# Two blocks of a transformer on one core: the low parts of three weight pieces and of one output piece are made earlier in VectorE's order

## The reference

```python
h = rms_norm_2(x, attn_norm_w[layer])
proj = h @ w_in[layer]
a_q, a_i, a_zf, a_zb, a_g, b_u, c_q, c_k, c_v = jnp.split(proj, SPLIT_POINTS, axis=-1)
o_a = hgrn2_mixer(a_q, a_i, a_zf, a_zb, a_g, lb_all[layer])      # recurrent, 4 heads
o_b = fourier_mixer(b_u)
o_c = dilated_attention_mixer(c_q, c_k, c_v, positions)           # 8 heads of 64
x = x + jnp.concatenate([o_a, o_b, o_c], axis=-1) @ w_out[layer]
h = rms_norm_2(x, mlp_norm_w[layer])
x = x + jnp.square(jax.nn.relu(h @ w_up[layer])) @ w_down[layer]
```

## Time and profile before

| | |
|---|---|
| median of 3 runs | 3080.66 us (3077.87 to 3081.01) |
| the profiled execution, its own time | 3081.01 us |
| span in its trace | 3079.2 us |
| TensorE (PE) busy | 2894.8 us, 94% |
| its weight loads (PEld) busy | 2291.1 us, 74% |
| VectorE (DVE) busy | 2159.4 us, 70% |
| ScalarE (ACT) busy | 1631.3 us, 53% |
| GpSimd (POOL) busy | 161.7 us, 5% |

### The profile page before, as it was taken

One profiled execution on the slowest core, in us unless ns is written; L12 is line 12 of the kernel. 1 busy time (PEld: TensorE's weight loads), 2 busy tenths in 40 slices (PEclk: granted clock), 3 DMA queues, 4 the chain that ended last, 5 costly groups with the idle time before them and its releaser, 6 DMA issues. The chain is left out here.

```text
span 3079.2 us, 40916 instructions
## 1 busy us (share of the span) xinstructions
PE 2894.8 (94%) x13474; PEld 2291.1 (74%) x13474; DVE 2159.4 (70%) x3016; ACT 1631.3 (53%) x2149; POOL 161.7 (5%) x120
## 2 busy tenths in 40 slices
PE   7988987899999999999997799899999998999998
PEld 6746666788888888888885676588887766688887
DVE  5477666999999999999996666554454466554444
ACT  5233553788888888888884435332232334342222
POOL 0000550000000000000002000000000000000000
PEclk9965586999999999999997899999999999999999
DMA  6167674899999999999997321233232321233222
GB/s 237 55 227 252 214 279 170 339 381 381 390 389 387 389 379 383 390 388 387 382 372 283 111 62 35 72 101 102 76 110 96 103 69 33 88 92 103 96 79 93
DMA packets 292110, 660.07 MB, mean 214 GB/s; under 512 B 21306, under 2 KB 145994, under 8 KB 291988
## 3 DMA queue, kind: packets, MB, share of 16 engines
q1 hardware_dynamic: 276178, 603.54, 53.1%
q0 software_dynamic: 10272, 37.04, 3.2%
q10 hardware_dynamic: 5538, 17.87, 1.5%
HBM read 582.86 MB, written 75.50 MB: 214 GB/s over the span
## 5 line engine op out<-in xcount | busy, mean ns | idle before, releaser
L1358 DVE TENSOR_TENSOR weights_low<-pieces,weights_high 128x1024 fp32r<-128x1024 f32 x768 | 891.3, 1219 | 73.8 <-ACT weights_high L1351 64.1
L1351 ACT ACTIVATE weights_high<-pieces 128x1024 fp32r<-128x1024 f32 x768 | 804.8, 1061 | 204.0 <-PE banks L261 203.3
L259 PE MATMUL banks<-weights_high,xT_high 128*128 128x512 f32 x1024 | 403.7, 394 | 1.3 <-DVE weights_low L1358 1.3
L260 PE MATMUL banks<-weights_low,xT_high 128*128 128x512 f32 x1024 | 400.2, 391 | 0.0
L261 PE MATMUL banks<-weights_high,xT_low 128*128 128x512 f32 x1024 | 400.0, 391 | 0.0
L2218 ACT ACTIVATE weights_high<-pieces 128x1024 fp32r<-128x1024 f32 x192 | 200.7, 1053 | 322.2 <-DMA pieces<-in_w_up 249.6
L2222 DVE TENSOR_TENSOR weights_low<-pieces,weights_high 128x1024 fp32r<-128x1024 f32 x192 | 233.5, 1223 | 115.2 <-ACT weights_high L2218 89.9
L259 PE MATMUL banks<-hT_high,weights_high 128*128 128x512 f32 x704 | 281.9, 400 | 2.8 <-DVE hT_low L3244 2.8
L260 PE MATMUL banks<-hT_low,weights_high 128*128 128x512 f32 x704 | 274.5, 390 | 0.0
L261 PE MATMUL banks<-hT_high,weights_low 128*128 128x512 f32 x704 | 274.5, 390 | 0.0
L259 PEld LDWEIGHTS banks<-weights_high,xT_high 128*128 128x128 f32 x1024 | 193.1, 189 | 53.0 <-issue 13.6
(11 more groups left out here) (459 smaller groups left out, 4658.5 us busy)
## 6 DMA issues: line engine op xcount, KB each, us to landing
pieces<-in_w_mlp SPq DMA_DIRECT2D x768, 512.0 KB, 7.5
expert_out<-mask SPq DMA_DIRECT2D x32, 1536.0 KB, 14.7
pieces<-in_w_up SPq DMA_DIRECT2D x64, 512.0 KB, 3.9
pieces<-in_w_down SPq DMA_DIRECT2D x64, 512.0 KB, 3.3
pieces<-in_w_in SPq DMA_DIRECT2D x56, 512.0 KB, 4.8
pieces<-in_w_ada SPq DMA_DIRECT2D x48, 512.0 KB, 5.9
expert_out<-y ACTq DMA_DIRECT2D x32, 512.0 KB, 7.6
pieces<-in_w_out SPq DMA_DIRECT2D x16, 512.0 KB, 4.5
```

The source lines that it names most:

```text
L259: nc.tensor.matmul(out, a[0], b[0], start=start, stop=False)
L260: nc.tensor.matmul(out, a[0], b[1], start=False, stop=False)
L1351: self.core.nc.scalar.activation(self.hi[:, c % E_PARTS, :], self.raw[:, c % E_RAW, :], ACT.Copy).then_inc(self.high.sem, 1)
L1358: self.core.nc.vector.tensor_tensor(self.lo[:, c % E_PARTS, :], self.raw[:, c % E_RAW, :], self.hi[:, c % E_PARTS, :], ALU.subtract).then_ ...
```

## The change

In slots 17, 18 and 19 (where `in_splits` isn't empty and there is something to pass) VectorE's `split` moves ahead of `normalise_probs(i - 1)` and `low_values(i - 2)`. In slot 16 these two do not occur with h = 0. Behind slot 23, `split(layer, P_OUT)` moves ahead of `low_values(layer, 14)`. That makes four moves in a layer and eight in all. ScalarE's list, TensorE's list and the DMAs stay as they are, and nothing is added or removed.

```diff
@@ VectorE, slots 16 to 23, for h in range(2)
                             if s == 23 and h == 0:
                                 rec_gate(layer, 0)
+                            if h == 0:
+                                for p in in_splits[s]:
+                                    split(layer, p)
                             if i >= 1:
                                 normalise_probs(layer, i - 1)
                             if i >= 2:
                                 low_values(layer, i - 2)
-                            if h == 0:
-                                for p in in_splits[s]:
-                                    split(layer, p)
                             if s == 17 and h:
                                 carry(layer, 0)
@@ VectorE, behind slot 23
                     normalise_probs(layer, 15)
+                    split(layer, P_OUT)
                     low_values(layer, 14)
-                    split(layer, P_OUT)
                     split(layer, P_OUT + 1)
```

## The result

| | us |
|---|---|
| kernel before, median of 5 runs | 3080.66 (3075.52 to 3081.20) |
| changed kernel, median of 5 runs | 3105.62 (3095.62 to 3109.59) |
| ratio of the runs, 95% interval | 1.0091 (1.0076 to 1.0106) |
| profiled execution: time, span | 3105.49, 3103.7 |

The forecast was 3105.9 with a range of 3098 to 3112. The ratio stands for 28 us and its interval for 23 to 33 us. The two spans differ by 3103.7 - 3079.2 = 24.5 us. Single times of the changed kernel scatter widely: the record lists 14 executions of it, from 3095.62 to 3113.65 us, with a median of 3107.6 us. That the forecast meets the median of five to 0.3 us is luck.

The account below looks back on a forecast made before the run. The prediction took TensorE, busy for 94% of the span, to bound the kernel. Waits of 15.8 + 2.3 = 18.1 us plus 6.8 us of clock gave 24.9 us over 3081.0, hence 3105.9 us, range 3098 to 3112.

Parts of the forecast that it names:

- Who waits, and for what: Slots 17 to 19: TensorE's transposes need low_values; in slot 17 any delay beyond some 0.6 us becomes TensorE idle time.
- Nothing gained by listing the split earlier: Slots 17 to 19: VectorE's split still waits for ScalarE's half, in slot 17 until 1846.49, with normalising and low_values behind it.
- 2.63 us a move, 15.8 us: Slots 17 to 19, both layers: transposes start about 2.63 us late at each of six moves, together 15.8 us.
- 0.08 us of overlap, 1.46 us, 0.15 us: VectorE's back-to-back overlap; first reciprocal to end of low_values without waits; end of low_values to start of a waiting TensorE.
- 1.14 us behind slot 23: Behind slot 23: low_values(14) is pushed back 1.14 us with TensorE already waiting; 2.3 us for two layers.
- Nothing absorbed: After the moved splits: VectorE and TensorE are late together and gaps keep their width, so the whole 18.1 us counts.
- The clock, 6.8 us: Behind the six new stalls of 2.48 us: TensorE's lowered clock costs 1.58 us at five in seven, 6.8 us in all.
- The share of five in seven: Old trace, two mixers: five of seven stalls of 2.29 to 2.58 us had a lowered clock; share applied to new stalls.
- rival 1: The new TensorE stalls come, but the clock holds behind all or nearly all of them: 3099.1 us; chance 0.16.
- Rival 2: All six new TensorE stalls and the two old ones spared before lose clock: 3111.8 us; chance 0.08.
- rival 3: The delay of slots 17 to 19 is absorbed, only the moves behind slot 23 remain: 3083.3 us; chance 0.04.
- rival 4: First output product behind slot 23: TensorE takes up its piece sooner, 0.20 us a layer, 3080.6 us; chance 0.02.

Follow-up runs that it names:

- number 3: Kernel before, with VectorE's split placed between normalise_probs and low_values in slots 17 to 19, old order behind slot 23; 3091.44 us, ratio 1.0034.
- Number 4: Changed kernel with ScalarE's half of the split moved ahead of exponents(i - 1) from slot 16 on, old order behind slot 23; 3084.64 us, ratio 1.0007.
- number 2: Kernel before, with only the split of P_OUT moved ahead of low_values(14) behind slot 23; 3085.69 us, ratio 1.0010.
- Number 1: Changed kernel with the old order restored behind slot 23, so only the moves in slots 17 to 19 remain; 3104.05 us, ratio 1.0063.
- number 5: Changed kernel with eight unused TensorE products put into each of the six new stalls; 3101.06 us, ratio 1.0062 to the kernel before.
- 6: Kernel before, with unused TensorE products put into stalls it already had, ahead of the transposes of units 0, 7 and 9 to 14; 3074.60 us, ratio 0.9983.
- number 7: Kernel before, with slot 16's three splits moved behind exponents(0) on ScalarE and behind normalise_probs(0) on VectorE; 3070.08 us, ratio 0.9967.

## Why the prediction was right, point by point

- **Who waits, and for what.** The step that decided was that the transposes wait for low_values(i - 2), not only for the normalising. It is shown: number 3 pushes low_values back alone and TensorE is late by 1.43 us.
- **Nothing gained by listing the split earlier.** VectorE waited 2.57, 1.94 and 1.64 us for ScalarE's half in the three slots of layer 0. Number 4 takes that wait away, and with it most of the cost.
- **2.63 us a move, 15.8 us.** The four distances that hold nothing else grew by 2.60, 2.64, 2.61 and 2.62 us. The durations behind the forecast (0.08 us of overlap, 1.46 us, 0.15 us) all came from rows of before.
- **1.14 us behind slot 23.** It measured 1.14 and 1.12 us; number 2 alone, 1.12 in both layers. It ran into a stall that was there already, so there was no room.
- **Nothing absorbed.** Seven distances a layer are unchanged to 0.1 us in sum. Number 1 keeps its 2.6 us a move to the end of the mixer as well.
- **The clock, 6.8 us.** In the trace it comes to 25.25 - 15.8 - 2.3 = 7.2 us. Behind the six new stalls it was 6.2 us from four (1.54 us each, forecast 1.58), and about 1 us came from old stalls, which the forecast had put at zero. That idle time is what brings the lowered clock is shown by numbers 5 and 6. The share of five in seven became four in six. So the price was right. That the whole term fits is in part luck: 0.6 us too much behind the new stalls stand against 1 us too little behind the old ones, and the share rested on seven cases. The ten traces have 58 stalls of 2.41 to 2.58 us in front of turn_probs, and behind 49 of them the clock was lowered in the next 4 us. By that share, as an estimate, the term would have been 6 x 49/58 x 1.58 = 8.0 us. The Trainium skill ("TensorE: Matmul & The Clock Gate", section "Why this matters for your kernels") advises against idle gaps only when they are longer than these stalls. By that advice the term would be nothing, and these runs do not agree with it.
- **The rivals.** That the clock holds behind all new stalls (rival 1) describes number 5, not the changed kernel. Rival 2 came true in part: of the two old stalls that had been spared, one fell (unit 9 to 10 of layer 0, 0.91 us), while the other shrank from 2.29 to 1.66 us and kept its clock; but two of the six new ones kept theirs too. That the delay is absorbed (rival 3) is refuted by the distances and by number 1, and that an earlier piece is used earlier (rival 4) by layer 1 of number 2.

## What to carry to other kernels

In an engine's strictly ordered list, place first what the bounding engine waits for soonest, and a split with four slots to spare after it. A move is priced by three timelines: how long the moved instruction waits at its new place, how long it runs, and how much room the waiting engine had. When idle times of some 2.5 us appear on TensorE, add the lowered clock behind them; and where such idle times exist already, look for the instruction in front that could stand elsewhere, as in slot 16, before filling them.

## What had not been expected of the hardware

- The clock behind stalls of equal length is not the same. Of stalls of 2.46 to 2.48 us, slot 17's kept 1.00 and slot 18's fell to 0.63 in the changed kernel; with number 1 it was the other way round (0.56 and 1.00). Behind these new stalls both layers of one execution agreed; behind old ones they didn't always: of the 2.41 us in front of unit 9, layer 0 kept 1.00 and layer 1 fell to 0.63 in the kernel before. What decides it stays open; it wasn't tried.
- Length sorts the stalls well all the same. Of the 58 of 2.41 to 2.58 us in the ten traces 49 were followed by a lowered clock. Of the 86 of 1.18 to 1.66 us in front of units 1 to 14 none was (for unit 15 see number 3).
- Eight unused products of 1.98 us in a stall of 2.5 us were enough to keep the clock at 1.00, with 0.63 to 0.67 us of idle time left, in six of six cases.
- Single times scatter far more than the mixers do. The same transposes (the last turn_qk of layer 0) start at 1828.81 us in the changed kernel, 1830.02 in the one before, 1833.88 in number 1 and 1825.90 in number 7, although nothing that is listed ahead of them differs. From there on, distances that neither the change nor the clock touches repeat to 0.05 us. For a change of a few us, paired distances tell more than whole times.
